# A two-tile decoder step after an expert layer: more of tile 0's second feed-forward under tile 1's expert rows, its down products one at a time in tile 1's gaps

## The chip, the cores and the metric

The kernel runs on one core of a Trainium2 chip, as one program. The metric is the device time of one execution in microseconds; of several executions the median is taken. PE is TensorE, DVE VectorE, ACT ScalarE, POOL GpSimd and SP SyncE. All numbers are 32-bit floats.

## The reference, cut to what matters

There are 256 tokens of width 1024, in two tiles of 128 (tile 0, tile 1). The first block mixes them (retention and attention) and then applies product-key experts: each token picks 16 of 16384 experts in each of 8 heads, and each pick reads a row of `peer_u` and a row of `peer_v`:

```python
u = expert_u[experts]
vsel = expert_v[experts]
act = jax.nn.gelu(jnp.einsum('thkd,td->thk', u, hb), approximate=False)
return jnp.einsum('thk,thkd->td', gate * act, vsel)
```

The second block has two layers. Layer 0 is a short convolution, cross attention to a memory, and a SwiGLU feed-forward (width 2816); layer 1 is block attention, memory attention and a feed-forward again; a norm ends it:

```python
for l in range(DEPTH_2):
    h = rms_norm_2(x, norm_mix[l])
    if l < N_A:
        x = x + short_conv_mixer(h, conv_w_in[l], conv_w[l], conv_w_out[l])
    else:
        x = x + moba_attention(h, ...)
    x = x + mem_cross_attention(...)
    x = x + swiglu(rms_norm_2(x, norm_ffn[l]), ffn_w_gu[l], ffn_w_down[l])
...
return rms_norm_2(x, norm_final)
```

Apart from the block attention of tile 1, which reads keys and values of tile 0, and the convolution's two last columns of tile 0, the tiles don't need each other.

## The kernel before

**The picks.** A pick fetches one row of u and v for each of 128 tokens, 1 MB, with an indirect DMA on POOL's queue (L1602) into one of eight row slots. 16 picks form a group g; picks 0 to 127 are tile 0's, 128 to 255 tile 1's. DVE takes the dot of u with the token (L2064), ACT makes gelu, weight and a small diagonal from it (L1546, L1552, L1559), PE adds diagonal times v into two banks of its own (L1140), and the row slot is free for pick n + 8.

**The layer work.** The second block is cut into steps: `turn`, the norm's transpose of x; `cin`, `q0`, `gu0`, `bk` and so on, products of a tile with one weight block of 2 MB (`layer_unit`, L974: eight matmuls 128x512, each two instructions in the trace); `zturn`, `qturn`, `pturn`, `fturn`, transposes (`layer_turns`, L981); `scores`, `values`, `probs`, `taps`, `rope`, `final`. `gu1 0` to `gu1 10` are the gate and up products of layer 1, eleven blocks; six `fturn1` transposes of their result follow between them; `dn1 0` to `dn1 5` are the down products (L1053), three blocks for each half of x's 1024 columns, the last of each half 1.5 MB. The digit behind a step's name is its layer, the argument its block; a 0 or 1 before it its tile.

**The order.** `STEPS` lists all steps with a cost in us and a lag. The planner (`LAYER_FIRST`, `LAYER_LAST`, `PICK_US`) spreads tile 0's steps over the pick pairs of tile 1, from pair 136 on, at 3.7 us of listed cost for one pick: `PICK_WORK[n]` is what stands before pick pair n on PE, and behind the diagonals of that pair on ACT. DVE does the dots of four picks and then the layer work of both their pairs. Steps planned past pair 252 are `LATE`. That is all of tile 0 from turn ffn1 on. After the rows come tile 1's steps, in order (`AFTER_ROWS`); ahead of each with a lag stands the next late step of tile 0, and the down products of one half go together.

**The weights.** SP loads the blocks in the order in which PE takes them (`SEQUENCE`, L596), into three slots of 2 MB; a slot is free again at the semaphore of the unit that read it last.

**The banks.** Every result of a step is a unit; units take four banks in turn, and PE opens a unit when the one four before it has been read by its engine, DVE or ACT (`UNITS`, `open_unit`). The three down products of one half add up in one bank, and DVE adds it to x once (L2171).

**Names the steps below use.** `add_experts` (L2074) adds the expert sum to x; `tile_x_wait` makes a turn wait for the last addition to x; `f_tok` are the two halves of gated product that `fturn` transposes to `fT`; `oT` holds the attention result for `mo`, `probs` the softmax.

Of the kernel before, what the change touches and what calls it, by code (L numbers as in the profile page):

```python
# [19 lines left out]
D = 1024  # L20
KC = D // P
# [7 lines left out]
MH, BH = 4, 8  # L29
DFF = 2816  # L30
FC = DFF // P
# [171 lines left out]
def feed_steps(l):  # L203

    steps = [(f"turn ffn{l}", 2, 2), (f"root ffn{l}", 0, 0)]
    for j in range(11):
        steps.append((f"gu{l} {j}", 7, 0 if j else 2))
        if j >= 2 and j % 2 == 0:
# [6 lines left out]
         + [("turn blk", 2, 2), ("root blk", 0, 0), ("bk 0", 7, 2), ("bk 1", 7, 0), ("bq 0", 7, 0), ("bq 1", 7, 0), ("bv 0", 7, 0), ("rope 0", 0, 0),  # L215
            ("bv 1", 7, 0), ("kturn 0", 2, 2), ("bqturn 0", 2, 0), ("bscores 0", 2, 2), ("bprobs 0", 0, 2), ("bpturn 0", 2, 2), ("bvalues 0", 3, 2),
            ("bo 0", 7, 2), ("bo 1", 7, 0)] + memory_steps(1) + feed_steps(1) + [("final 0", 0, 2)])
LAYER_FIRST, LAYER_LAST, PICK_US = 136, 252, 3.7
UNDER_ROWS, LATE = [], []
_at, _load = LAYER_FIRST, float(LAYER_FIRST)  # L220
for _w, _us, _lag in STEPS:
    _at = max(_at + _lag, 2 * int(_load // 2))
    _load = max(_load, _at) + _us / PICK_US
    if _at <= LAYER_LAST and not LATE:
        UNDER_ROWS.append(_w)
        PICK_WORK.setdefault(_at, []).append("layer 0 " + _w)
    else:
        LATE.append((_w, _us))
AFTER_ROWS = []
for _w, _us, _lag in STEPS:  # L230
    while _lag and LATE:
        _late, _late_us = LATE.pop(0)
        AFTER_ROWS.append((0, _late))
        if _late_us > 2 and not (_late[:2] == "dn" and _late[-1] not in "25"):
            break
    AFTER_ROWS.append((1, _w))
AFTER_ROWS += [(0, _w) for _w, _ in LATE]
SEQUENCE = [(0, _w) for _w in UNDER_ROWS] + AFTER_ROWS


def units_of(work):

    kind, what = work.split()[:2]
    if kind == "query":
        return [(what, "A")]
    if kind == "keys":
        return [("k" + what, "D")]
    if kind == "regroup":
        return [("g" + what, "D")]
    if kind in ("row", "mean"):  # L250
        return [(what, "D")]
    if kind == "out" and what == "1":
        return [("o1a", "D"), ("o1b", "D")]
    if kind == "repeat":
        return [(f"e{what}a", "A"), (f"e{what}b", "D")]
    if kind == "mkey":
        return [("mk" + what, "A")]
    if kind == "mvalue":
        return [("mv" + what, "A")]
    if kind == "layer":  # L260
        t, step, arg = work.split()[1:]
        late = t == "1"
        return [(n.format(t=t, a=arg, s=step, l=step[-1]), e) for n, e in
                {"turn": [("t{a}{t}0", "D"), ("t{a}{t}1", "A")], "cin": [("ci{t}{a}", "D" if arg in "45" else "A")], "zturn": [("z{t}0", "D"), ("z{t}1", "A")],
# [4 lines left out]
                 "dn": [("dn{l}{t}" + str(int(arg) // 3), "D")] if arg in "25" else [],  # L269
                 "bk": [("bk{t}{a}", "A")], "bq": [("bq{t}{a}", "A")], "bv": [("bv{t}{a}", "A")],  # L270
                 "kturn": [("bkt{t}0", "D"), ("bkt{t}1", "A")], "bqturn": [("bqt{t}0", "D"), ("bqt{t}1", "A")],
                 "bscores": [("bs{t}%d" % i, "D") for i in range(4 if late else 2)],
                 "bpturn": [("bp{t}%d" % i, "DA"[i % 2]) for i in range(4 if late else 2)],
                 "bvalues": [("bw{t}0", "D"), ("bw{t}1", "A")], "bo": [("bo{t}{a}", "D")]}.get(step.rstrip("01"), [])]
    return []
# [21 lines left out]
def units_freed(name, who):  # L297

    return sum(w == who for _, w in UNITS[:unit(name) + 1])
# [22 lines left out]
def build_program(nc, a, out):  # L322
# [5 lines left out]
    with ExitStack() as ctx:  # L328
# [5 lines left out]
        def sem(name):  # L334
            if name not in sems:
                sems[name] = ctx.enter_context(nc.semaphore(name))
            return sems[name]
# [85 lines left out]
        def blocks(v):  # L423
            return v.rearrange("p (k n) -> p k n", n=P)

        def tile_buffers(t):

            def at(t0, t1, n=1024):
                where, c = (t0, t1)[t]
                return where[:, c:c + n]  # L430
# [8 lines left out]
            if t:  # L439
# [2 lines left out]
            heads = 8 * (t + 1)  # L442
            return TileBuffers(
                squares=work, hT=blocks(at((hT_all, 1024), (arena, 3072))), kvT=blocks(first), b_tok=low, z_tok=high, q_tok=low,
                zT=at((h2_all, 0), (arena, 6144), 1040).rearrange("p (k n) -> p k n", k=KC), cvT=blocks(high), qT=blocks(high), oT=blocks(low),
                probs=[v.rearrange("p (h n) -> p h n", h=MH) for v in (first, later)], probs_low=work,
                pT=work.rearrange("p (h k n) -> p h k n", h=MH, k=2),
                sg=[v[:, 0:512].rearrange("p (b n) -> p b n", b=2) for v in (first, later)], f_tok=[v[:, 512:1024] for v in (first, later)], fT=fT, fT4=fT4,
                k_tok=low, bq_tok=high, kq=both.rearrange("p (g n) -> p g n", g=16), rot=work[:, 0:512].rearrange("p (s g n) -> p s g n", s=2, g=16),
# [88 lines left out]
        for name, i, _ in plan:  # L538
            step, t = name[:-1], name[-1]
            if step in ("cin", "cout", "bk", "bq", "bv", "bo"):  # L540
                last_unit[name, i] = {"cin": "ci", "cout": "co"}.get(step, step) + f"{t}{i}"
            elif step[:-1] in ("q", "mo", "gu") and step[-1] in "01":
                last_unit[name, i] = {"q": "lq", "mo": "lo", "gu": "gu"}[step[:-1]] + f"{step[-1]}{t}{i}"
            elif step[:-1] == "dn" and i % 3 == 2:
                last_unit[name, i] = f"{name}{i // 3}"

        def part_read(i):

# [6 lines left out]
        def wait_released(eng, n):  # L555

            name, i, _ = plan[n]
            if name == "mod":
                eng.wait_ge(turn_ready, turn(f"m{i}") + 1)
            elif (name, i) == ("out_again", 1):  # L560
                eng.wait_ge(sem("out_half_used"), 1)
            elif (name, i) in last_unit:
                eng.wait_ge(unit_ready, unit(last_unit[name, i]) + 1)
            elif (name, i) in middle:
                eng.wait_ge(sem("piece_used"), middle.index((name, i)) + 1)
            else:
                assert name[:2] == "dn"
                eng.wait_ge(sem(f"{name}_used"), 2 * (i // 3) + i % 3 + 1)

        def tile_x_wait(eng, t, name, u):  # L570

            if name == "conv":
                eng.wait_ge(experts_added[t], u + 1)
            else:
                eng.wait_ge(unit_free["D"], units_freed({"mem0": "co", "ffn0": "lo0", "blk": "dn0", "mem1": "bo", "ffn1": "lo1", "final": "dn1"}[name] + f"{t}{u}", "D"))

        @block.sync
        def _(sp):
# [26 lines left out]
        def _(pe):  # L605
# [378 lines left out]
            def layer_step(t, step, arg):  # L984
# [49 lines left out]
                                    m = mm(b[:, c - i * 512:c - i * 512 + P], V[:, k, c:c + P], v.pT[:, h, k], start=(k == 0), stop=(k == 1))  # L1034
                        m.then_inc(unit_ready, 1)
                elif kind == "mo":
                    layer_unit(f"lo{l}{t}{arg}", (f"mo{l}{t}", int(arg)), v.oT, f"v{l}{t}0", f"v{l}{t}1")
                elif kind == "gu":
                    layer_unit(f"gu{l}{t}{arg}", (f"gu{l}{t}", int(arg)), v.hT, f"tffn{l}{t}0", f"tffn{l}{t}1")
                elif kind == "fturn":  # L1040
# [2 lines left out]
                    layer_turns(f"ft{l}{t}{m}", [v.f_tok[l][:, c * P:(c + 1) * P] for c in range(4 if m < 5 else 2)])  # L1043
                elif kind == "dn":
                    half, c = divmod(int(arg), 3)
                    if c == 0:
                        open_unit(f"dn{l}{t}{half}", steps_ahead=True)
                    b = bank[unit(f"dn{l}{t}{half}") % 4]
                    w = weights(piece[f"dn{l}{t}", int(arg)])
                    for k in range(8 * c, min(8 * c + 8, FC)):  # L1050
                        if half == 0 and k % 4 == 0:
                            unit_read(f"ft{l}{t}{k // 4}")
                        m = mm(b[:, :], v.fT[k], slot8[w][:, k % 8], start=(k == 0), stop=(k == FC - 1))  # L1053
                    if c == 2:
                        open_unit(f"dn{l}{t}{half}", opened_ahead=True)
                    m.then_inc(unit_ready if c == 2 else sem(f"dn{l}{t}_used"), 1)
                elif kind in ("bk", "bv", "bq"):
                    layer_unit(f"{kind}{t}{arg}", (f"{kind}{t}", int(arg)), v.hT if kind == "bq" else v.kvT, f"tblk{t}0", f"tblk{t}1")
                elif kind == "kturn":
# [105 lines left out]
        def _(act):  # L1165
# [275 lines left out]
            def layer_step(t, step, arg):  # L1441
# [55 lines left out]
                elif kind == "pturn":  # L1497
                    unit_copy(f"pt{l}{t}1", v.probs_low[:, 512:1024])
                elif kind == "values":
                    unit_copy(f"v{l}{t}1", v.oT[:, 4:8])  # L1500
                elif kind == "gu":
                    i, ss, ms, sd, rs = tile_stats(t, f"ffn{l}")
                    j = int(arg)
# [104 lines left out]
        def _(dve):  # L1608
# [504 lines left out]
            def layer_step(t, step, arg):  # L2113
# [48 lines left out]
                elif kind == "bturn":  # L2162
                    for u in range(2):
                        name = f"b{t}{u}"
                        tt(v.cvT[:, 4 * u:4 * u + 4], v.cvT[:, 4 * u:4 * u + 4], unit_in(name)[:, :].rearrange("p (c n) -> p c n", c=4),
                           ALU.mult).then_inc(unit_free["D"], 1)
                elif kind in ("cout", "mo", "bo") or kind == "dn" and arg in "25":
                    half = int(arg) if kind != "dn" else int(arg) // 3
                    name = {"cout": f"co{t}", "mo": f"lo{l}{t}", "bo": f"bo{t}", "dn": f"dn{l}{t}"}[kind] + str(half)
                    c = slice(half * 512, (half + 1) * 512)  # L2170
                    tt(x[:, t, c], x[:, t, c], unit_in(name)[:, :], ALU.add).then_inc(unit_free["D"], 1)  # L2171
                elif kind == "qturn":
                    unit_copy(f"qt{l}{t}0", v.qT[:, 0:4])
# [10 lines left out]
                elif kind == "pturn":  # L2184
                    unit_copy(f"pt{l}{t}0", v.probs_low[:, 0:512])
                elif kind == "values":
                    unit_copy(f"v{l}{t}0", v.oT[:, 0:4])
                elif kind == "gu":
                    i, ss, ms, sd, rs = tile_stats(t, f"ffn{l}")
                    j = int(arg)  # L2190
# [113 lines left out]
```

## Time and profile before

| | us |
|---|---|
| median of 3 runs | 1830.45 |
| lowest, highest | 1827.85, 1831.81 |
| the profiled execution | 1836.24 |
| its span in the trace | 1834.4 |
| mean granted clock of PE | 0.946 |
| PE busy in it | 1623.2 (88%) |
| DVE busy | 738.1 (40%) |
| ACT busy | 484.9 (26%) |
| moved by DMA | 595.21 MB |

The profiled execution stands 5.8 us above the median of the others. Times in rows are microseconds from the start of its span. A row of the timeline is a run of like instructions: start, length, engine and line, what it writes and reads, how many; in brackets, the idle time of the engine just before it and what ended it. A matmul overlaps the next, so the time of a step is read from its start to the start of the one behind it.

### The profile page before, as it was taken

The numbers are of one execution on the slowest core, as the hardware profiler recorded it, in microseconds if no ns is written. First come the engines' busy times: TensorE is split into PE (matmuls) and PEld (weight loads), VectorE is DVE, ScalarE is ACT, GpSimd is POOL, SyncE is SP. The second block draws the span as 40 slices with busy tenths as digits, with TensorE's granted clock in tenths as the row PEclk, the third lists the DMA queues.
The fourth block names the chain that finished last, engine by engine and source line by source line (L and its number), as shares of the span: only waits on it lengthen the run. The fifth ranks groups of instructions, "written<-read, shape, count | busy, mean of one in ns | idle before, by whom it ended". The sixth has DMA issues, their size and how long they took to land.

```text
span 1834.4 us, 15459 instructions
## 1 busy us (share of the span) xinstructions
PE 1623.2 (88%) x5460; PEld 755.6 (41%) x5460; DVE 738.1 (40%) x1784; ACT 484.9 (26%) x1267; POOL 277.5 (15%) x268
## 2 busy tenths in 40 slices
PE   6998998498569998898799999789999999989998
PEld 3444464174134442233333333244445444455443
DVE  3653146866584555746635445451101010031000
ACT  3311223323222323323443323332112011122110
POOL 1000002333243323322312222320000000000000
PEclk8998999799889998899899999899999999999999
DMA  9545337999999999999999999996776677764674
GB/s 354 193 156 183 121 143 312 412 377 417 421 388 371 399 421 417 413 421 421 417 375 420 422 420 422 420 387 227 288 281 257 263 304 280 301 237 183 255 295 183
DMA packets 94956, 595.21 MB, mean 324 GB/s; under 512 B 7024, under 2 KB 7024, under 8 KB 28192
## 3 DMA queue, kind: packets, MB, share of 16 engines
q1 hardware_dynamic: 56576, 319.28, 44.9%
q0 software_dynamic: 37584, 270.75, 36.1%
q10 hardware_dynamic: 720, 4.19, 0.6%
q8 instruction: 44, 0.72, 0.2%
q14 instruction: 32, 0.26, 0.0%
HBM read 593.15 MB, written 1.05 MB: 324 GB/s over the span
## 4 chain that ended last, share of the span: by engine, by line
PE 76%; DMA 9%; DVE 8%; ACT 4%; issue 2%; POOL 1%; DVEq 0%; SPq 0%; ACTq 0%; POOLq 0%
PE bank L974 35%; PE bank L1140 9%; PE bank L1053 8%; PE bank L684 6%; DMA arena<-in_peer_rows,pidx 6%; PE bank L946 3%; DVE arena L2064 3%; DMA ring<-in_w_mod 2%; PE bank L937 2%; PE bank L761 2%; PE bank L981 2%; PE bank L738 1%; PE bank L781 1%; PE bank L1034 1%; PE bank L656 1%
## 5 line engine op out<-in xcount | busy, mean ns | idle before, releaser
L1602 POOL DMA_INDIRECT arena<-in_peer_rows,pidx x256 | 272.6, 1065 | 921.2 <-PE bank L1140 603.3
L1140 PE MATMUL bank<-arena,keep 128*32 128x512 f32 x1024 | 277.6, 691 | 128.5 <-ACT keep L1559 128.4
L2064 DVE SCALAR_TENSOR_TENSOR arena<-arena,ring 128x1024 f32<-128x1024 f32 x256 | 304.8, 1221 | 165.1 <-DMA arena<-in_peer_rows,pidx 163.8
L974 PE MATMUL bank<-ring,arena 128*128 128x512 f32 x736 | 319.3, 592 | 1.1 <-issue 1.1
L974 PE MATMUL bank<-ring,hT_all 128*128 128x512 f32 x544 | 242.4, 601 | 4.9 <-issue 2.6
L974 PEld LDWEIGHTS bank<-ring,arena 128*128 128x128 f32 x736 | 138.7, 190 | 170.8 <-issue 170.8
L1140 PEld LDWEIGHTS bank<-arena,keep 128*32 128x32 f32 x1024 | 52.3, 119 | 300.2 <-ACT keep L1559 168.6
L974 PEld LDWEIGHTS bank<-ring,hT_all 128*128 128x128 f32 x544 | 102.4, 192 | 137.3 <-issue 137.2
L2171 DVE TENSOR_TENSOR x_all<-x_all,bank 128x512 f32<-128x512 f32 x24 | 16.5, 687 | 224.2 <-PE bank L1053 125.7
L1546 ACT ACTIVATE pf<-pf 128x2 f32<-128x2 f32 x128 | 25.8, 201 | 302.9 <-DVE arena L2064 302.7
L684 PE MATMUL bank<-ring,hT_all 128*128 128x512 f32 x192 | 89.0, 621 | 3.0 <-DVE hT_all L1679 3.0
L1053 PE MATMUL bank<-ring,arena 128*128 128x512 f32 x176 | 75.9, 592 | 0.0
L1559 ACT ACTIVATE keep<-keep,pf 128x32 f32<-128x32 f32 x256 | 68.2, 313 | 4.2
L2194 DVE SCALAR_TENSOR_TENSOR arena<-bank,stat,arena 128x256 f32<-128x256 f32 x22 | 10.6, 484 | 137.9 <-ACT arena L1508 137.9
L1552 ACT ACTIVATE pf<-pf,grouped 128x1 f32<-128x1 f32 x256 | 61.4, 287 | 4.2
L761 PE MATMUL bank<-hT_all,ring 128*128 128x128 f32 (+1 forms) x384 | 60.6, 317 | 0.3 <-ACT hT_all L1175 0.3
L684 PEld LDWEIGHTS bank<-ring,hT_all 128*128 128x128 f32 x192 | 38.0, 201 | 51.3 <-issue 51.3
L974 PE MATMUL bank<-ring,s_all 128*128 128x512 f32 x128 | 55.9, 595 | 3.4 <-issue 3.4
L761 PEld LDWEIGHTS bank<-hT_all,ring 128*128 128x128 f32 x384 | 55.0, 197 | 8.9 <-issue 5.6
L937 PE MATMUL bank<-mem_all,ring 128*128 128x256 f32 x256 | 58.3, 386 | 0.0
L946 PE MATMUL bank<-ring,mem_all 128*128 128x512 f32 x128 | 57.0, 598 | 0.0
L1053 PE MATMUL bank<-ring,s_all 128*128 128x512 f32 x128 | 56.2, 595 | 0.1
(365 smaller groups left out, 1551.3 us busy)
## 6 DMA issues: line engine op xcount, KB each, us to landing
ring<-in_weights SPq DMA_DIRECT2D x126, 2048.0 KB
ring<-in_w_mod SPq DMA_DIRECT2D x12, 2048.0 KB
ring<-in_w_in SPq DMA_DIRECT2D x6, 2048.0 KB
ring<-in_weights SPq DMA_DIRECT2D x8, 1024.0 KB
arena<-in_peer_rows,pidx POOLq DMA_INDIRECT x256
ring<-in_weights SPq DMA_DIRECT2D x8, 512.0 KB
mem_all<-in_b_mod POOLq DMA_DIRECT2D x3, 512.0 KB, 9.7
hT_all<-in_xT ACTq DMA_DIRECT2D x1, 1024.0 KB, 7.6
```

What stands on the lines that cost most here:

```text
L684: m = mm(b[:, :], src[:, k, t * P:(t + 1) * P], slot8[w][:, k], start=(k == 0), stop=(k == KC - 1))
L761: m = mm(b[:, s * n:(s + 1) * n], slot8[w][:, k, c:c + P], hT[:, k, cols_of], start=(k == 0), stop=(k == KC - 1))
L937: m = mm(bk[:, b * TOK:(b + 1) * TOK], slot8[w][:, k, (2 * half + b) * P:(2 * half + b + 1) * P], memT[l][:, k], start=(k == 0), stop=(k = ...
L946: m = mm(b[:, :], memT[l][:, k, t * P:(t + 1) * P], slot4[w][:, k % 4, half * 512:(half + 1) * 512], start=(k == 0), stop=(k == KC - 1))
L974: m = mm(b[:, :], src[:, k], slot8[w][:, k], start=(k == 0), stop=(k == KC - 1))
L981: i = tr(b[:, c * P:(c + 1) * P], src, ident)
L1053: m = mm(b[:, :], v.fT[k], slot8[w][:, k % 8], start=(k == 0), stop=(k == FC - 1))
L1140: m = mm(acc[b][r:r + 32, :], diag[n % 8], vslot[n % SLOTS][:, b * 512:(b + 1) * 512], start=(n % 128 < 4), stop=(n % 128 >= 124))
L1552: m = f(pw2[:, c + k:c + k + 1], pgel2[:, c + k:c + k + 1], ACT.Copy, scale=grouped[:, g % 4, i % 4, 1, i // 4:i // 4 + 1])
L1559: f(diag[n % 8], eq32, ACT.Copy, scale=pw2[:, c + k:c + k + 1]).then_inc(sem("diag_ready"), 1)
L1602: nc.gpsimd.indirect_dma_start(out=row_in[n % SLOTS], out_offset=None, in_=a["peer_rows"], in_offset=bass.IndirectOffsetOnAxis(ap=pidx[:, ...
L2064: stt(uslot[n % SLOTS], uslot[n % SLOTS], 1.0, h2g[n % 4], ALU.mult, ALU.mult, accum_out=pact2[:, 16 * (g % 2) + k:16 * (g % 2) + k + 1]). ...
```

## The change

`LAYER_LAST` goes, `PICK_US` is 5.2, and the planner places every step of tile 0 under the rows but the six `dn1` and `final`. All steps from pair 144 on stand closer: turn mem0 before pair 152 instead of 156, turn blk before 196 instead of 212, and turn ffn1, all of gu1 and fturn1 before pairs 234 to 252. After the rows the seven steps left stand where `FILLS` says: one down product each ahead of tile 1's turn conv, cin 2, turn mem0, probs0, turn ffn0 and turn blk, and the norm ahead of tile 1's gu1 3. Each down product, of both tiles and layers, is now a unit with a bank and an addition to x of its own. `oT` and `probs` of layer 1 take other parts of the buffers.

```diff
-LAYER_FIRST, LAYER_LAST, PICK_US = 136, 252, 3.7
-UNDER_ROWS, LATE = [], []
+LAYER_FIRST, PICK_US = 136, 5.2
+UNDER_ROWS, DOWN = [], [f"dn1 {c}" for c in range(6)]
 _at, _load = LAYER_FIRST, float(LAYER_FIRST)
 for _w, _us, _lag in STEPS:
     _at = max(_at + _lag, 2 * int(_load // 2))
     _load = max(_load, _at) + _us / PICK_US
-    if _at <= LAYER_LAST and not LATE:
+    if _w not in DOWN + ["final 0"]:
+        assert _at < 256
         UNDER_ROWS.append(_w)
         PICK_WORK.setdefault(_at, []).append("layer 0 " + _w)
-    else:
-        LATE.append((_w, _us))
+FILLS = {"turn conv": ["dn1 0"], "cin 2": ["dn1 1"], "turn mem0": ["dn1 2"], "probs0 0": ["dn1 3"], "turn ffn0": ["dn1 4"], "turn blk": ["dn1 5"],
+         "gu1 3": ["final 0"]}
 AFTER_ROWS = []
 for _w, _us, _lag in STEPS:
-    while _lag and LATE:
-        _late, _late_us = LATE.pop(0)
-        AFTER_ROWS.append((0, _late))
-        if _late_us > 2 and not (_late[:2] == "dn" and _late[-1] not in "25"):
-            break
-    AFTER_ROWS.append((1, _w))
-AFTER_ROWS += [(0, _w) for _w, _ in LATE]
+    AFTER_ROWS += [(0, _fill) for _fill in FILLS.get(_w, ())] + [(1, _w)]
...
-                 "dn": [("dn{l}{t}" + str(int(arg) // 3), "D")] if arg in "25" else [],
+                 "dn": [("dn{l}{t}{a}", "D")],
...
                 elif kind == "dn":
                     half, c = divmod(int(arg), 3)
-                    if c == 0:
-                        open_unit(f"dn{l}{t}{half}", steps_ahead=True)
-                    b = bank[unit(f"dn{l}{t}{half}") % 4]
                     w = weights(piece[f"dn{l}{t}", int(arg)])
-                    for k in range(8 * c, min(8 * c + 8, FC)):
+                    ks = range(8 * c, min(8 * c + 8, FC))
+                    b = open_unit(f"dn{l}{t}{arg}")
+                    for k in ks:
                         if half == 0 and k % 4 == 0:
                             unit_read(f"ft{l}{t}{k // 4}")
-                        m = mm(b[:, :], v.fT[k], slot8[w][:, k % 8], start=(k == 0), stop=(k == FC - 1))
-                    if c == 2:
-                        open_unit(f"dn{l}{t}{half}", opened_ahead=True)
-                    m.then_inc(unit_ready if c == 2 else sem(f"dn{l}{t}_used"), 1)
+                        m = mm(b[:, :], v.fT[k], slot8[w][:, k % 8], start=(k == ks[0]), stop=(k == ks[-1]))
+                    m.then_inc(unit_ready, 1)
...
-                elif kind in ("cout", "mo", "bo") or kind == "dn" and arg in "25":
-                    half = int(arg) if kind != "dn" else int(arg) // 3
+                elif kind in ("cout", "mo", "bo", "dn"):
+                    half = int(arg) // (3 if kind == "dn" else 1)
...
+                    if kind == "dn" and arg not in "03":
+                        copied(f"dn{l}{t}{int(arg) - 1}")
                     tt(x[:, t, c], x[:, t, c], unit_in(name)[:, :], ALU.add).then_inc(unit_free["D"], 1)
```

## Rows read from the trace of the kernel before

**Rows 1.** The page: busy time, and DMA in forty slices of the span
```profile
PE 1623.2 (88%) x5460; PEld 755.6 (41%) x5460; DVE 738.1 (40%) x1784; ACT 484.9 (26%) x1267; POOL 277.5 (15%) x268
...
DMA  9545337999999999999999999996776677764674
GB/s 354 193 156 183 121 143 312 412 377 417 421 388 371 399 421 417 413 421 421 417 375 420 422 420 422 420 387 227 288 281 257 263 304 280 301 237 183 255 295 183
```

**Rows 2.** Windows: under tile 1's rows, after them, and a part of the first
```profile
core 0: us, PE busy (x) PEld busy (x) DVE busy (x) ACT busy (x) POOL busy (x), PEclk, DMA share, GB/s
...
750.70:1251.70 501.00, 449.55 (x1401) 180.78 (x1397) 243.22 (x580) 173.61 (x470) 120.31 (x112) 0.95 0.98 406
1251.70:1834.40 582.70, 557.90 (x1540) 268.17 (x1538) 71.16 (x164) 94.65 (x193) 0.00 (x0) 0.99 0.69 260
...
1075.20:1184.00 108.80, 93.79 (x293) 37.37 (x291) 51.94 (x115) 35.24 (x105) 26.91 (x24) 0.91 1.01 421
```

**Rows 3.** Windows: the last 22 us of the stretch under the rows
```profile
1230.00:1240.00 10.00, 10.00 (x47) 6.26 (x46) 5.36 (x9) 3.03 (x11) 0.00 (x0) 0.91 0.46 190
1240.00:1252.00 12.00, 12.00 (x42) 4.81 (x42) 1.49 (x3) 0.00 (x0) 0.00 (x0) 1.00 0.54 189
```

**Rows 4.** DMA issues by line, with their size
```profile
ring<-in_weights SPq DMA_DIRECT2D x126, 2048.0 KB
```

**Rows 5.** Waits from 750 to 1252 us: total, times, longest
```profile
PE bank L1140 <- ACT keep L1559: 44.0, 16, 6.7
```

**Rows 6.** Timeline of PE under the rows: cout, two pick pairs, bpturn
```profile
817.09 13.97 PE L974 MATMUL bank<-ring,s_all 128*128 128x512 f32 x32 [2.92 <-issue]
...
911.99 3.63 PE L1140 MATMUL bank<-arena,keep 128*32 128x512 f32 x8 [6.67 <-ACT keep L1559]
...
1158.43 1.97 PE L981 MATMUL bank<-keep,s_all 128*128 128x128 f32 x8 [2.71 <-DVE s_all L2232]
...
1234.01 1.91 PE L1140 MATMUL bank<-arena,keep 128*32 128x512 f32 x8
```

**Rows 7.** Timeline of PE after the rows, where tile 0's late steps stand
```profile
1251.65 1.09 PE L981 MATMUL bank<-keep,x_all 128*128 128x128 f32 x8
1255.33 8.80 PE L974 MATMUL bank<-ring,hT_all 128*128 128x512 f32 x16 [2.59 <-issue]
1263.97 1.04 PE L981 MATMUL bank<-keep,x_all 128*128 128x128 f32 x8
...
1306.92 7.03 PE L974 MATMUL bank<-ring,arena 128*128 128x512 f32 x16
1313.79 7.03 PE L974 MATMUL bank<-ring,hT_all 128*128 128x512 f32 x16
...
1321.53 0.60 PE L981 MATMUL bank<-keep,s_all 128*128 128x128 f32 x4
1322.97 7.10 PE L974 MATMUL bank<-ring,hT_all 128*128 128x512 f32 x16 [0.84 <-DVE s_all L2194]
...
1414.75 3.73 PE L1034 MATMUL bank<-arena,mem_all 128*128 128x128 f32 x32
```

**Rows 8.** Timeline of PE in tile 1's layer 1, with nothing of tile 0
```profile
1665.52 0.60 PE L981 MATMUL bank<-keep,x_all 128*128 128x128 f32 x4
...
1667.11 13.97 PE L974 MATMUL bank<-ring,arena 128*128 128x512 f32 x32
1680.92 0.60 PE L981 MATMUL bank<-keep,arena 128*128 128x128 f32 x4
...
1682.35 3.69 PE L1018 MATMUL bank<-mem_all,arena 128*128 128x256 f32 x16
...
1689.58 5.29 PE L1034 MATMUL bank<-arena,mem_all 128*128 128x128 f32 x32
1694.70 13.90 PE L974 MATMUL bank<-ring,arena 128*128 128x512 f32 x32
```

**Rows 9.** The page: DVE's additions of a product to x
```profile
L2171 DVE TENSOR_TENSOR x_all<-x_all,bank 128x512 f32<-128x512 f32 x24 | 16.5, 687 | 224.2 <-PE bank L1053 125.7
```

More of the change, by code:

```diff
@@ L444, in tile_buffers @@
                 squares=work, hT=blocks(at((hT_all, 1024), (arena, 3072))), kvT=blocks(first), b_tok=low, z_tok=high, q_tok=low,
-                zT=at((h2_all, 0), (arena, 6144), 1040).rearrange("p (k n) -> p k n", k=KC), cvT=blocks(high), qT=blocks(high), oT=blocks(low),
-                probs=[v.rearrange("p (h n) -> p h n", h=MH) for v in (first, later)], probs_low=work,
+                zT=at((h2_all, 0), (arena, 6144), 1040).rearrange("p (k n) -> p k n", k=KC), cvT=blocks(high), qT=blocks(high), oT=[blocks(low), blocks(high)],
+                probs=[v.rearrange("p (h n) -> p h n", h=MH) for v in (first, low)], probs_low=work,
                 pT=work.rearrange("p (h k n) -> p h k n", h=MH, k=2),
@@ L541, in build_program @@
                 last_unit[name, i] = {"cin": "ci", "cout": "co"}.get(step, step) + f"{t}{i}"
[L542 to L545, printed above, removed]
+            elif step[:-1] in ("q", "mo", "gu", "dn") and step[-1] in "01":
+                last_unit[name, i] = {"q": "lq", "mo": "lo"}.get(step[:-1], step[:-1]) + f"{step[-1]}{t}{i}"
         def part_read(i):
@@ L563, in wait_released @@
                 eng.wait_ge(unit_ready, unit(last_unit[name, i]) + 1)
-            elif (name, i) in middle:
+            else:
                 eng.wait_ge(sem("piece_used"), middle.index((name, i)) + 1)
-            else:
-                assert name[:2] == "dn"
-                eng.wait_ge(sem(f"{name}_used"), 2 * (i // 3) + i % 3 + 1)
         def tile_x_wait(eng, t, name, u):
@@ L574, in tile_x_wait @@
             else:
-                eng.wait_ge(unit_free["D"], units_freed({"mem0": "co", "ffn0": "lo0", "blk": "dn0", "mem1": "bo", "ffn1": "lo1", "final": "dn1"}[name] + f"{t}{u}", "D"))
+                eng.wait_ge(unit_free["D"], units_freed({"mem0": "co{t}{u}", "ffn0": "lo0{t}{u}", "blk": "dn0{t}{d}", "mem1": "bo{t}{u}", "ffn1": "lo1{t}{u}",
+                                                              "final": "dn1{t}{d}"}[name].format(t=t, u=u, d=3 * u + 2), "D"))
         @block.sync
@@ L1036, in layer_step @@
                 elif kind == "mo":
-                    layer_unit(f"lo{l}{t}{arg}", (f"mo{l}{t}", int(arg)), v.oT, f"v{l}{t}0", f"v{l}{t}1")
+                    layer_unit(f"lo{l}{t}{arg}", (f"mo{l}{t}", int(arg)), v.oT[l], f"v{l}{t}0", f"v{l}{t}1")
                 elif kind == "gu":
@@ L1499, in layer_step @@
                 elif kind == "values":
-                    unit_copy(f"v{l}{t}1", v.oT[:, 4:8])
+                    unit_copy(f"v{l}{t}1", v.oT[l][:, 4:8])
                 elif kind == "gu":
@@ L2166, in layer_step @@
                            ALU.mult).then_inc(unit_free["D"], 1)
-                elif kind in ("cout", "mo", "bo") or kind == "dn" and arg in "25":
-                    half = int(arg) if kind != "dn" else int(arg) // 3
-                    name = {"cout": f"co{t}", "mo": f"lo{l}{t}", "bo": f"bo{t}", "dn": f"dn{l}{t}"}[kind] + str(half)
+                elif kind in ("cout", "mo", "bo", "dn"):
+                    half = int(arg) // (3 if kind == "dn" else 1)
+                    name = {"cout": f"co{t}", "mo": f"lo{l}{t}", "bo": f"bo{t}", "dn": f"dn{l}{t}"}[kind] + arg
                     c = slice(half * 512, (half + 1) * 512)
+                    if kind == "dn" and arg not in "03":
+                        copied(f"dn{l}{t}{int(arg) - 1}")
                     tt(x[:, t, c], x[:, t, c], unit_in(name)[:, :], ALU.add).then_inc(unit_free["D"], 1)
@@ L2186, in layer_step @@
                 elif kind == "values":
-                    unit_copy(f"v{l}{t}0", v.oT[:, 0:4])
+                    unit_copy(f"v{l}{t}0", v.oT[l][:, 0:4])
                 elif kind == "gu":
```

## The prediction

> **What bounds the kernel now.** I read the page first, then split the span where the structure of the kernel does. The page says that PE is busy for 1623.2 us, 88% of the span, so the idle 12%, some 210 us, is all that can be won by moving work; and that from the fifteenth to the twenty-sixth of forty slices the transfers run at one flat rate, 413 to 422 GB/s but for one slice at 375 [rows 1]. So there are two regimes. The windows give them apart. From 750.7 us (pick pair 138, where tile 0's layer work starts) to 1251.7 us (the last pick) PE is busy 449.55 of 501.0 us and the DMA engines 0.98 of the time: this stretch is bound by transfers. From there to the end PE is busy 557.90 of 582.7 us and DMA only 0.69, at 260 GB/s: this one is bound by PE [rows 2]. The reader should see that PE has about 51 us free in the first, and DMA about a third of its time free in the second. The change moves eleven 2 MB blocks, with their products, out of the stretch that has DMA to spare into the one that has none. Whether it pays is a comparison of two prices for the same work, its bytes and its PE time.
>
> The chain of waits agrees: in the first stretch PE waits 44.0 us for the diagonals of ACT, which wait for DVE's dots, which wait for rows [rows 5]. In the second, units follow each other at 6.87 us, the distance between the start of one and the start of the next [rows 7].
>
> **The second stretch, what leaves.** Turn ffn1 and gu1 0 take from 1251.65 to 1263.97, 12.3 us, with 2.59 of idle among them [rows 7]. Ten further gu1 units are 10 x 6.87 = 68.7 us. The six transposes of tile 0's f_tok cost, from the start of each to the start of the work behind it, 1.44 us (1321.53 to 1322.97 [rows 7]) where DVE is awaited; four more places of this kind give 1.32, 1.32, 0.44 and 1.83 us, 6.35 us together. Sum 87.4 us. The six products of dn1 stay in this stretch and keep their time.
>
> **The second stretch, what comes back.** The moved work had filled tile 1's waits. The same steps of tile 1's other layer have no filler and price them [rows 8]. Turn mem runs 1.59 us from its start to that of q (1665.52 to 1667.11) against the 0.87 us of eight transposes without a wait, so +0.72; bturn is built alike, +0.72. Qturn takes 1.43 us (1680.92 to 1682.35), +0.56, and pturn, with dn1 3 now ahead of it, +0.56 likewise. Values take 5.12 us (1689.58 to 1694.70) where they took some 3.6 us filled (the 3.73 us row of [rows 7]), +1.55. Together 4.1 us. Turn blk gains a filler, -0.6. I take +3.5; its bounds are 0 (the new fillers cover all) and about 7 (bturn as dear as cout's 2.92 us wait [rows 6], values with another 1 us). That tile 1's first turn waits for the experts' sum costs nothing: dn1 0, one unit of 6.87 us, covers it, and it is the 2.59 us that gu1 0 paid before. The stretch shrinks by 87.4 - 3.5 = **84 us**.
>
> **The first stretch, what is added.** Eleven blocks of 2.097 MB [rows 4] are 23.1 MB. At 421 GB/s, the rate that holds there [rows 1], they cost **54.8 us**. In PE time the same work is 11 x 6.87 + 6.35 = 81.9 us with its turns, more than the 51 us of idle, so PE alone asks for at least 31 us more; the bytes ask for more and decide. That needs both to fit: 449.6 + 82 = 532 us of PE work in a stretch of about 556 us is 96%, which is tight, but the 532 holds picks at the lower clock (3.63 us for a pair after 6.67 us of idle, against 1.91 us [rows 6]), which shrink as the waits for rows do.
>
> Two corrections. First the tail: behind the last row's landing DMA does 190 GB/s for 22 us [rows 3], 12 us of lost transfer. In the new order PE has two units, three short turns and four pick pairs, 13.7 + 1.5 + 7.6 = 23 us, behind the last row's issue, where it had 26; I take -3 us. Second the order: DVE reads units only after the dots of a group of four rows, so a step whose input DVE made in the same group waits for two rows more. Reading the planned places, 11 such steps stood under the rows before, and 17 do now, since steps now fall one pair apart (zturn, cout, q, scores, pturn, mo, gu0 0, two of fturn0, bk, kturn, bvalues, turn mem1, values1, turn ffn1, two of fturn1). PE's two longest waits at the old ones are 2.92 us at cout and 2.71 us at bpturn [rows 6], and the fturns in such places carry no idle in PE's timeline; at a little under 1 us each for six more, +5 us. The bounds of the whole term: below, every idle moment of DMA used up, (203.4 + 23.1) MB / 421 = 538 us, +37; above, PE's 51 us of idle all kept and its 82 us added, +82. I take 54.8 - 3 + 5 = **+57**, nearer to the lower end because transfers ran at 0.98 in this stretch already.
>
> Here a rule of the Trainium skill speaks against the change. The page's slices show 421 GB/s for hundreds of microseconds on end [rows 1]. DMA: Bandwidth & Descriptors, Where 436 GB/s comes from, says that for transfers from HBM the limit is the HBM side, about 358 GB/s for a core; by it the 23.1 MB would be an estimated 64 us and not 55, and the gain 9 us smaller. The trace disagrees with it as a ceiling, and the measured rate is used.
>
> **Edits at nothing.** Sixteen more additions of a down piece to x, eight of them under the rows, are 16 x 0.687 = 11 us of DVE [rows 9], which is idle half of the first stretch and seven eighths of the second; the very last addition is the same as before. Uncovered, the eight under the rows would cost 5.5 us. Weight slots of dn come free at the same matmul as before. Each piece now takes a bank of its own, and a bank is asked for again four units later, some 27 us. Final 0 puts about 3 us of ACT and 2.5 us of DVE under one gu1 unit of tile 1 that lasts 6.87 us; its stores stay at the end of SP's queue. POOL issues the same 256 rows. The moved blocks pass nothing on SP's queue but each other, and share the engines with the rows, which is the 54.8 us.
>
> **Sum.** -84 + 57 = -27 us. The profiled execution took 1836.2 us (span 1834.4), so a profiled run of the new kernel should be near 1809; it stands 5.8 us above the median of the three runs, 1830.45, and against that the forecast is **1803 us**. A measurement of this kernel can tell about 0.2% (3.7 us) from no change.
>
> **The rivals.**
> *Idle transfers are used up (0.12).* Denser PE work frees slots evenly and DMA never stops but for a short tail: about +42 instead of +57, so 1788. For it: PE's clock rises when waits vanish. Against: what idle there was came when PE was the slower one, which will be more common.
> *PE's idle stays (0.10).* The waits under the rows are of order and not of bytes, and the 82 us simply add: -84 + 82 = -2, so 1828; a little of it used gives 1825. For it: 96% use of two engines with eight row slots and three weight slots between them. Against: DMA at 1.01 for stretches of 109 us on end [rows 2].
> *The groups of four bind; slower (0.08).* PE stands at the 17 steps listed, units behind it cannot run, weight slots stay full and DMA stops too. It decides from a total of 43 us, 2.5 us a step (27 + 5 + some 11 paid now). With 4.4 us each, between the 2.9 of the longest such wait and the 6.67 us of the longest wait for a diagonal [rows 6], it is 17 x 4.4 - 11 = 64 us in place of 5: 1862. Against it: the fturns in such places show no wait now.
> *The rate falls with more weights in the mix (0.05).* Two slices, the twelfth and thirteenth, gave 388 and 371 GB/s with DMA at nine tenths or more [rows 1]; at 371 the bytes cost 62 us: 1810. The skill's 358 points this way.
> *The change does less than it says (0.03).* Tile 1's bare waits cost four times my 3.5 us, since fillers stand in the wrong places: 1814.
> The forecast itself has 0.62, with its own range 1791 to 1816.
>
> **Numbers.** The range 1787 to 1822 takes in the forecast, the first rival, the last two and part of the second; what is left out is most of the second and the slower one, under 2 in 10. Faster by over 0.2% (below 1826.8): 0.62 + 0.12 + 0.05 + 0.03 and 0.04 of the second, 0.86. Same: the rest of it, 0.06. Slower: 0.08.
>
> **What the new profile would show.** The last pick moves from 1251 to about 1308 us; the stretch before it holds 226 MB at over 400 GB/s with PE idle down from 51 to some 30 us; the rest lasts about 499 us with PE at 96% or more and DMA lower than before; picks of 3.6 us become rarer. Wrong it would be if that stretch grows past 575 us with DMA below 0.93 (order, not bytes), or if the rest is over 510 us (bare waits).

## The result, and the profile after

The kernel after takes 1821.8 us in the median against 1832.2 for the kernel before: ratio 0.994, interval 0.9928 to 0.9952, some 11 us faster. The forecast was 27 us. One of its 18 executions took 5606.5 us and is left out of the ratio. The profiled execution took 1821.5 us, where the one of before stands 4 us above its median. The page of the kernel after, the parts that answer to [rows 1]:

```profile
span 1819.7 us, 15512 instructions
...
PE 1620.8 (89%) x5460; PEld 754.2 (41%) x5460; DVE 748.3 (41%) x1800; ACT 502.0 (28%) x1279; POOL 288.1 (16%) x268
...
DMA  9545237999999999999899999999977577754774
GB/s 355 200 154 185 115 152 307 406 383 417 421 395 372 402 420 416 421 421 391 344 386 401 421 421 386 421 405 421 369 268 281 211 293 271 301 228 185 264 291 183
```

PE's work is the same, its idle time fell by 12 us. The flat rate of DMA now has a hole at the nineteenth to twenty-second slice (391, 344, 386, 401), where the kernel before had one slice at 375. I cut the span at the same steps as before: turn conv of tile 0 at 748.6 us (752.5 before), the last pick at 1317.4 (1251.7). The windows, with the columns of [rows 2], are the whole stretch under the rows, the rest of the span, and then the stretch by tile 0's parts. Each part is named after the turn it begins with: conv, mem0, ffn0, blk, mem1, ffn1.

```profile
748.60:1317.40 568.80, 527.67 (x1602) 216.83 (x1600) 250.26 (x598) 204.11 (x506) 123.32 (x112) 0.96 0.98 401
1317.40:1819.70 502.30, 479.67 (x1334) 233.31 (x1332) 73.71 (x162) 79.48 (x165) 0.00 (x0) 0.98 0.67 252
748.60:823.00 74.40, 72.55 (x213) 29.88 (x211) 34.45 (x93) 18.97 (x55) 14.78 (x14) 0.99 1.01 421
823.00:893.40 70.40, 57.49 (x204) 25.59 (x202) 36.48 (x93) 25.00 (x68) 18.76 (x16) 0.93 0.92 363
893.40:1047.90 154.50, 148.20 (x413) 58.57 (x411) 62.82 (x154) 55.15 (x119) 30.67 (x28) 0.98 0.98 400
1047.90:1150.50 102.60, 90.56 (x285) 36.91 (x283) 53.85 (x129) 36.25 (x106) 26.43 (x22) 0.92 0.99 405
1150.50:1213.40 62.90, 56.92 (x204) 25.58 (x202) 33.55 (x77) 23.82 (x68) 15.70 (x16) 0.92 1.01 412
1213.40:1317.40 104.00, 101.96 (x296) 40.29 (x294) 29.12 (x54) 44.92 (x92) 17.00 (x16) 0.98 0.97 402
```

Counted from turn conv in both, the stretch grew from 499.2 to 568.8 us, +70 where +57 was forecast, and the rest fell from 582.7 to 502.3, -80 where -84 was forecast: -11 in all, which is what the medians say. Inside the stretch PE's busy time rose by 80 us (447.75 in the same cut of before) and its idle time fell only from 51 to 41 us. The part mem0 stands out: PE is idle for 13 of 70 us and DMA runs at 363 GB/s. Both wait there, so a third must be late.

It is DVE. Waits in the stretch of the kernel after, and below them the one of before that compares with the second row (total, times, longest):

```profile
PE bank L1128 <- ACT keep L1547: 41.1, 14, 7.0
DVE arena L2052 <- DMA arena<-in_peer_rows,pidx: 19.2, 8, 7.8
```
```profile
DVE arena L2064 <- DMA arena<-in_peer_rows,pidx: 61.0, 32, 4.0
```

PE waits for the picks' diagonals nearly as long as before (41.1 against 44.0 us [rows 5]), but DVE waits for rows only a third as long (19.2 against 61.0). So most rows have landed, and their dots are late. The longest of PE's waits, at pick pair 160, in the timeline of the kernel after (start, length, engine, line; in brackets idle time and what ended it):

```profile
847.38 0.69 DVE L1629 COPY s_all<-bank 128x512 f32<-128x512 f32 x1 [8.42 <-PE bank L972]
...
853.88 0.69 DVE L2166 TENSOR_REDUCE small<-bank 128x2 f32<-128x512 f32 x1 [5.80 <-PE bank L1009]
...
856.41 0.17 DVE L1969 TENSOR_SCALAR ptop<-ptop 128x16 uint32<-128x16 uint32 x1
...
860.45 0.29 DVE L1986 TENSOR_TENSOR s_all<-comb,keep 128x128 f32<-128x128 f32 x1
860.66 1.22 DVE L2052 SCALAR_TENSOR_TENSOR arena<-arena,ring 128x1024 f32<-128x1024 f32 x1
...
863.82 0.53 ACT L1547 ACTIVATE keep<-keep,pf 128x32 f32<-128x32 f32 x2
...
864.40 3.63 PE L1128 MATMUL bank<-arena,keep 128*32 128x512 f32 x8 [7.00 <-ACT keep L1547]
868.80 0.94 POOL L1590 DMA_INDIRECT arena<-in_peer_rows,pidx  x1 [8.45 <-PE bank L1128]
```

DVE waits 8.4 us for PE in qturn and 5.8 us in scores, the layer work of the two pairs of one group; then it does 4.2 us of picking for a later group (L1969 to L1986); then the dots of rows 160 to 163, without a wait for them. PE has nothing left from 857.4 to 864.4, and the pick behind it runs at 3.63 us instead of 1.91. POOL, which gets its slots from that pick, issues no row for 8.45 us. The DMA rate falls with it:

```profile
860.00:870.00 10.00, 5.59 (x20) 2.38 (x22) 7.66 (x21) 2.52 (x11) 1.30 (x2) 0.66 0.69 283
```

That is one place of the hole; the rest of it, up to 1000 us, is not traced to single waits here.

### The profile page after: what moved, and what is told of

It is laid out like the page before. It is cut to its first block, busy times and chain, and to the rows that moved or that the text cites. A ratio compares the mean times of both kernels' runs of the same rounds, so it can differ in the third digit from the quotient of the medians.

```text
span 1819.7 us, 15512 instructions
## 1 busy us (share of the span) xinstructions
PE 1620.8 (89%) x5460; PEld 754.2 (41%) x5460; DVE 748.3 (41%) x1800; ACT 502.0 (28%) x1279; POOL 288.1 (16%) x268
## 4 chain that ended last, share of the span: by engine, by line
PE 76%; DVE 9%; DMA 8%; ACT 4%; issue 2%; POOL 1%; DVEq 0%; SPq 0%; ACTq 0%; POOLq 0%
PE bank L965 34%; PE bank L1128 10%; PE bank L1043 8%; PE bank L675 6%; DMA arena<-in_peer_rows,pidx 6%; PE bank L937 3%; DVE arena L2052 3%; PE bank L928 2%; PE bank L752 2%; DMA ring<-in_w_mod 2%; PE bank L972 2%; PE bank L729 1%; PE bank L647 1%; PE bank L1025 1%; POOL arena L1590 1%
## 5 line engine op out<-in xcount | busy, mean ns | idle before, releaser
L1590 POOL DMA_INDIRECT arena<-in_peer_rows,pidx x256 | 283.2, 1106 | 979.2 <-PE bank L1128 662.7
L2161 DVE TENSOR_TENSOR x_all<-x_all,bank 128x512 f32<-128x512 f32 x40 | 27.5, 688 | 225.9 <-PE bank L1043 124.2
```

The costliest lines, as they stand in the source:

```text
L1590: nc.gpsimd.indirect_dma_start(out=row_in[n % SLOTS], out_offset=None, in_=a["peer_rows"], in_offset=bass.IndirectOffsetOnAxis(ap=pidx[:, ...
```

## The experiments

All are timed against the kernel before on the same chip, in five rounds. A ratio is to that kernel, and a difference in us between two runs is worked out from their ratios. First the two parts of the change that can stand alone, and the bytes.

**singles** and **dense_only**. Both have the products and buffers of the kernel after and the interleaving of the one before. singles keeps its planner; dense_only plans densely and stops at mo1 1, so that the last eleven pick pairs stand alone.

```diff
 # dense_only, against singles
-LAYER_FIRST, LAYER_LAST, PICK_US = 136, 252, 3.7
+LAYER_FIRST, LAYER_LAST, PICK_US = 136, 232, 5.2
```

> The kernel before with two parts of the change alone: each down product a unit of its own with its own addition to x, and the new places of oT and probs. The planner is that of before. Forecast's theory (edits at nothing): 1832 us, ratio to before 1.000 within 0.002. Rival (sixteen more additions and banks hold PE or DVE up, 0.7 us each where bare): up to 11 us more, 1843, ratio 1.006.

> Density alone: tile 0's steps stand as close under the rows as after the change (the same pairs up to mo1 1 before pair 232), but turn ffn1, gu1 and fturn1 stay behind the rows, interleaved as before, so that the last eleven pick pairs have no layer work. Bytes theory (the stretch under the rows costs its bytes at 421 GB/s): no more bytes, so 1832, ratio 1.000. Order theory (DVE stands in layer work while landed rows wait for their dots, and DMA stops): some 9 us of DMA idle more in the pairs up to 232, 1841, ratio 1.005.

Measured: singles 1832.8 us, ratio 0.9995 (0.9981 to 1.001): sixteen additions and the banks cost nothing, as forecast. dense_only 1849.1 us, ratio 1.0094 (1.0072 to 1.0116): 17 us slower with no more bytes under the rows. The windows show the stretch and the part of it up to 1200 us; below them are PE's waits for the diagonals up to there:

```profile
746.80:1262.40 515.60, 452.96 (x1397) 181.03 (x1395) 245.51 (x584) 170.59 (x464) 126.70 (x112) 0.93 0.97 397
746.80:1200.00 453.20, 415.13 (x1281) 172.52 (x1280) 219.83 (x542) 158.43 (x414) 107.63 (x96) 0.95 0.98 401
```
```profile
PE bank L1133 <- ACT keep L1552: 38.1, 12, 7.0
```

The stretch is 16.4 us longer than in the kernel before, with the same bytes within 1% (397 x 515.6 against 406 x 499.2). Its first 453 us look like those of the kernel after, the longest wait of 7.0 us included. Density has a price of its own, almost twice what I had expected of it here, and more than three times the 5 us of the forecast.

**half_gu1**. Of each gu1 block of tile 0 only half is loaded; the second half of these products uses old weights. PE does the same work.

```diff
+        if name == "gu10":
+            plan.append((name, i, [(a["weights"][n, 0], 0, RUN)]))
+            return
```

> The kernel after, but of each of the eleven gu1 blocks of tile 0 only the first half (1 MB) is loaded, so the second half of the product uses old weights: 11.5 MB less are moved under the rows, PE's work is the same. Bytes theory: 11.5 MB / 421 GB/s = 27 us less, 1794, ratio to before 0.979. PE-bound or order theory (PE is busy 102 of 104 us in the part that holds gu1): 0 to 6 us less, 1816 to 1821, ratio 0.991 to 0.994.

Measured: 1822.6 us, ratio 0.9936 (0.9912 to 0.9959), the same as the kernel after within the interval. The stretch, and the part with gu1:

```profile
751.30:1320.20 568.90, 526.70 (x1602) 217.33 (x1600) 249.91 (x598) 203.81 (x506) 122.48 (x112) 0.96 0.95 380
1216.00:1320.20 104.20, 102.17 (x296) 40.41 (x294) 29.11 (x54) 45.01 (x92) 16.95 (x16) 0.98 0.83 311
```

568.9 us in place of 568.8, 104.2 in place of 104.0, with DMA at 311 instead of 402 GB/s. So the bytes did not bind this part. PE did: it was busy for 102 of the 104 us.

**lead**. The kernel after with DVE's dots always one pick pair ahead of its layer work.

```diff
+            dotted = [0]
+
-            def dots(g, q):
-                for k in range(4 * q, 4 * q + 4):
-                    n = 16 * g + k
+            def dots(g, q, ahead=0):
+                for n in range(dotted[0], min(16 * g + 4 * q + 4 + ahead, 16 * PK)):
+                    dotted[0] = n + 1
+                    g, k = divmod(n, 16)
...
                     for n in (16 * g + 4 * q, 16 * g + 4 * q + 2):
+                        if g >= 8 and n % 4 == 2:
+                            dots(g, q, 2)
```

> The kernel after, with DVE's dots always one pick pair ahead of its layer work (from pick 128 on the two dots of the next pair come before the layer work of the second pair of each group of four rows), nothing else moved. Order theory: the picks' waits on ACT (41 us in 14 waits after the change, of which only 19 us of DVE's waits are for rows) shrink, the stretch of 569 us loses 8 to 12 us, 1811, ratio to before 0.989. Bytes theory: its bytes are the same, 1821, ratio 0.994.

Measured: 1798.9 us, ratio 0.9814 (0.9791 to 0.9838), the fastest kernel here that leaves nothing out, 34 us ahead of the one before and 23 of the one after; twice what I had expected. The stretch, and its parts ffn0, blk and ffn1, in lead; then its waits:

```profile
744.50:1296.60 552.10, 516.47 (x1603) 214.59 (x1601) 252.25 (x600) 205.80 (x511) 122.72 (x112) 0.98 1.01 415
...
886.40:1033.80 147.40, 145.47 (x413) 58.03 (x411) 62.72 (x154) 55.28 (x120) 30.10 (x28) 1.00 1.01 418
1033.80:1134.20 100.40, 87.11 (x285) 35.98 (x283) 52.60 (x126) 34.34 (x101) 23.70 (x22) 0.95 1.01 420
...
1195.00:1296.60 101.60, 100.52 (x297) 40.09 (x295) 27.96 (x54) 44.77 (x92) 17.86 (x16) 1.00 1.00 413
```
```profile
PE bank L1128 <- ACT keep L1547: 22.0, 7, 8.2
DVE arena L2055 <- DMA arena<-in_peer_rows,pidx: 50.7, 28, 4.0
```

PE's wait for diagonals is halved, and DVE waits for rows again: 31.4 of the 50.7 us stand in part blk, where DMA ran at 420 GB/s. Of the 17 us that the stretch lost, 11 are PE's busy time (527.7 to 516.5) and 6 its idle time. I had counted only the second kind. Most of the 11 is in the picks, as the windows of their line alone show, in the kernel after and in lead (PE and PEld only):

```profile
748.60:1317.40 568.80, 124.56 (x474) 23.48 (x472) 0.96 0.98 401
744.50:1296.60 552.10, 115.72 (x474) 22.61 (x472) 0.98 1.01 415
```

The remaining 6 of the 23 us lie outside the stretch: it starts 4.1 us earlier, and what follows it is 1.9 us shorter. That start scatters between 741 and 753 us over these kernels, so whether the 4.1 us are the early dots' is open.

**lead_before** and **lead_dense**: the same edit on the kernel before and on dense_only.

> The kernel before, with the dots one pick pair ahead as in lead. Order theory: in the kernel before the rows were the bottleneck (DVE waited 61 us for them), DMA idle was only 18 us of the stretch, so at most half of it comes back, 1824 to 1832, ratio 0.995 to 1.000; then the change on top of the early dots is worth 26 to 33 us, what its bytes and PE times had promised. Rival (the early dots are a gain of their own, whatever the placing): 22 us here too, 1811, ratio 0.988.

> Density alone (dense_only, 1.0094 of before), with the dots one pick pair ahead. Order theory: what density cost was DVE's place for the dots, and it goes: ratio to before 0.997 to 1.001, 1827 to 1834. Rival (steps one pair apart starve each other whatever DVE does): 1.005 or more stays, 1841.

Measured: lead_before 1829.9 us, 0.9979 (0.9965 to 0.9993); lead_dense 1831.1 us, 0.9988 (0.9972 to 1.0003). The early dots are worth 4 us without the change and 23 with it. With early dots in both, density costs one or two us instead of 17 (0.9988 against 0.9979). And the change is then worth 0.9814 / 0.9979 = 0.983, 30 us, the size that the forecast had given it.

**lead_half_gu1** and **lead_half_gu0**: is it the bytes that bind now? Lead, with half of each gu1 block of tile 0, or of each gu0 block, left out as in half_gu1.

> Lead, with only half of each gu1 block of tile 0 loaded (the second half of the product uses old weights). In lead the stretch moves 229 MB in 552 us, 544 us of it at 421 GB/s, and PE is busy 95.5 of the last 96.6 us. If bytes bind the whole stretch now: 11.5 MB / 421 GB/s = 27 us less, 1772, ratio to before 0.966. If the part with gu1 is bound by PE, whatever the bytes: 0 to 5 us less, 1794 to 1799, ratio 0.979 to 0.982.

> Lead, with only half of each of the eleven gu0 blocks of tile 0 loaded (the second half of those products uses old weights): 11.5 MB less in the part from tile 0's turn conv to its turn ffn1, which in lead took 450.5 us at 416 GB/s with PE busy 93% of it. If bytes bind this part in lead: 11.5 MB / 421 GB/s = 27 us at most, and as PE's own waits then come first, 10 to 25 us less than lead, 1774 to 1789, ratio to before 0.968 to 0.976. If order or PE binds it still, as in the part with gu1, where halving did nothing: 0 to 3 us, 1796 to 1801, ratio 0.980 to 0.983.

Measured: 1801.6 us, 0.9829 (0.9802 to 0.9855), and 1798.9 us, 0.98 (0.9779 to 0.9822): lead's time in both. For gu0 the expectation was 10 to 25 us if bytes bind and 0 to 3 if not, and DMA had run at 1.01 in its part; it is the second. The window of lead_half_gu0 about that part:

```profile
890.00:1045.00 155.00, 151.56 (x436) 60.51 (x433) 68.91 (x170) 61.80 (x136) 35.30 (x32) 1.00 0.92 358
```

DMA falls to 358 GB/s and the part keeps its length, 147.4 us from turn ffn0 to turn blk in both kernels. DMA at full rate was no bottleneck there; it was only never out of work. Nor did the saving reach the next, light part: from turn blk to turn mem1 lead takes 100.4 us and lead_half_gu0 100.7. My reading is that eight row slots and three weight slots can't hold it; no run changes the slots. So in the two product-heavy parts tested half of a block's bytes are free, and the block's price is PE's 6.87 us. No run takes bytes from a light part, and in lead's blk, with DMA at 420 GB/s and DVE waiting for rows, they may well bind.

**chosen_first**, **first138**: two other ways to change what stands ahead of the dots, on the kernel after. In chosen_first DVE's picking stands ahead of the group's layer work, not behind it. In first138 the planner starts one pair later, so every step of tile 0 stands one pick pair later on all engines.

```diff
 # chosen_first: these two blocks of DVE's loop change places
-                    for n in (16 * g + 4 * q, 16 * g + 4 * q + 2):
...
                     if 0 < g < 14:
                         if q < 2:
                             half_top(g + 2, q)
...
+                    for n in (16 * g + 4 * q, 16 * g + 4 * q + 2):
...
 # first138
-LAYER_FIRST, PICK_US = 136, 5.2
+LAYER_FIRST, PICK_US = 138, 5.2
```

> The kernel after, with DVE's picking of later experts (half_top, best_pairs, pair_rows, spread, 1.8 to 4.3 us for each group of four rows) moved ahead of the layer work of the group, where DVE waits for PE, instead of between it and the next dots. Order theory: the dots after six or seven of the groups come 2 to 4 us sooner, PE's wait of 7.0 us at pair 160 among them, 10 to 15 us in all, 1809, ratio 0.987. If only the position of the dots against the layer work counts, and not what stands between: 0 to 3 us, 1820, ratio 0.993.

> The kernel after, with every step of tile 0 one pick pair later (the planner starts at 138 instead of 136), so that each stands in the other half of its group of four rows. The forecast's rule counted steps whose input DVE makes in the same group: 17 before the shift, 16 after it; by it the time stays, 1821, ratio 0.993 to 0.995. If what counts is which light steps (turns, scores, probs) stand second in a group, ahead of the next dots, the waits move: the 7.0 us at pair 160 goes and others come, a difference of 4 us or more either way, with no bytes changed.

Measured: chosen_first 1814.0 us, 0.9889 (0.9868 to 0.991); first138 1812.9 us, 0.9887 (0.9866 to 0.9908). Each is 9 to 10 us faster than the kernel after, with the same bytes and the same products. PE's order is the same in chosen_first; in first138 the layer steps keep their order but stand between other picks. chosen_first lies between its two expectations, 10 to 15 us and 0 to 3. Their waits for diagonals, chosen_first and first138:

```profile
PE bank L1128 <- ACT keep L1547: 22.9, 9, 8.4
```
```profile
PE bank L1128 <- ACT keep L1547: 34.9, 12, 5.9
```

A shift by one pair is worth as much as most of the change. My count of steps that stand with their input in one group of four (17, and 16 after the shift) said that it was worth nothing. Which of the moved steps bring the 10 us is open.

**lead_fill3** and **both_fill3**. One place in the rest of the program: dn1 3 was meant to cover the softmax of tile 1's mem0. lead_fill3 is lead with dn1 3 behind DVE's scaling of the probabilities; both_fill3 is that with chosen_first's order as well. The timeline of PE there, in the kernel after:

```profile
1415.11 7.03 PE L1043 MATMUL bank<-ring,s_all 128*128 128x512 f32 x16
1423.65 1.38 PE L972 MATMUL bank<-keep,arena 128*128 128x128 f32 x8 [1.51 <-DVE arena L2173]
1425.13 5.44 PE L1025 MATMUL bank<-arena,mem_all 128*128 128x128 f32 x32
```

```diff
-         "probs0 0": ["dn1 3"]
+         "pturn0 0": ["dn1 3"]
```

> Lead, with tile 0's dn1 3 ahead of tile 1's pturn0 instead of ahead of probs0: PE's order stays the same, but DVE scales the probabilities during the product and adds it to x behind, where in the change it adds first and PE waits 1.5 us for the probabilities. Theory of the queue on DVE: 1.5 us less, 1797.5 against lead's 1799, near the limit of the measurement; in the trace the wait of 1.5 us between dn1 3 and pturn is gone. Rival (the product covers it anyway and the 1.5 us are of another wait): the same wait stays.

> All that helped: lead, chosen_first and dn1 3 behind DVE's scaling of the probabilities. In lead the stretch under the rows ran 544 of its 552 us at the full rate of DMA, so if the two cures are one, 1795 to 1799, ratio 0.980 to 0.982. If chosen_first's 9 us are of another kind and add up: 1789, ratio 0.976.

Measured: lead_fill3 1800.3 us, 0.9817 (0.9794 to 0.984), no difference in time that can be told from lead; both_fill3 1802.6 us, 0.983 (0.9805 to 0.9855), so what chosen_first brings does not add to lead. But the wait for DVE is gone in the timeline of lead_fill3:

```profile
1390.52 7.03 PE L1043 MATMUL bank<-ring,s_all 128*128 128x512 f32 x16
1397.39 1.04 PE L972 MATMUL bank<-keep,arena 128*128 128x128 f32 x8
1398.98 3.81 PE L1025 MATMUL bank<-arena,mem_all 128*128 128x128 f32 x32 [0.55 <-issue]
```

From the end of the product to values it is now 1.6 us, where lead and the kernel after have 3.15. PE's order is the same in both; DVE had the product's addition to x ahead of the probabilities in its queue, and waited for the product before it scaled them.

## Why the prediction was right or wrong

**The step that failed** is the first stretch's term, +57 = 54.8 - 3 + 5. It measured +70.

The term that was mis-sized is the +5 us for order. dense_only, which has the density and not the moved blocks, lengthened the stretch by 16.4 us (499.2 to 515.6). The kernel after stands another 53.2 us above it (568.8), where 54.8 - 3 = 52 was forecast for the moved blocks. So 11 of the missing 13 us are order's, as far as the two can be added.

The 54.8 us for the bytes came near in size by luck, for they were the price of something that did not bind. Half of the moved bytes taken away changed neither the part (104.2 against 104.0 us) nor the time. I had read the bound from a mean: DMA at 0.98 over 501 us. By parts it is another matter. Under the dense plan PE is busy for 72.6 of 74.4, 148 of 154.5 and 102 of 104 us of the product-heavy parts, and half of gu0's bytes are as free in lead as half of gu1's. The two prices nearly tie in the part with gu1: it moved 402 GB/s x 104.0 us = 41.8 MB, which at 421 GB/s is an estimated 99 us against PE's 102. What fits the runs is PE's account: 80 us more of busy time, as the prediction had it (82), less the idle time that the work took up, which was 10 us and not the 25 that +57 implies. Nor did the picks shrink, as the prediction thought: PE's time for them in the stretch was 123.9 us before and 124.6 after.

On order the prediction saw one half of the mechanism (DVE reads a unit only after the dots of its group) and looked for its price at the steps that wait for DVE. Most of it is paid at the picks: DVE waits for PE inside the layer work, and the dots of rows that have landed queue behind it. It costs 17 us in dense_only, nearly all of which the early dots give back, and lead is 23 us faster than the kernel after, against 4 us for the same edit on the kernel before. Nor did the count of places say anything, as the shift by a pair shows. The -3 us for the tail I could not check by itself.

**The rivals.** The one that PE's idle stays (1828, chance 0.10) was nearest in kind: 41 of 51 us stayed. The result, 11 us, lies between it and the forecast. In the rival of the groups of four the mechanism was partly right: in part mem0 DMA fell to 363 GB/s while PE and DVE waited for each other. But at 17 us it makes a smaller gain and not a slower kernel. Idle transfers weren't used up: 401 GB/s against 406. The rate did not fall by the mix of queues: slices at 420 and 421 GB/s still stand in the stretch, and part conv runs at 421. By that the Trainium skill's figure of some 358 GB/s (DMA: Bandwidth & Descriptors, Where 436 GB/s comes from) is again not the ceiling of this core; where 358 does appear, in lead_half_gu0, half of the block bytes had been left out of a part that ran at 418 with them.

**The second stretch** came near, -80 for -84. The filler of turn blk brought nothing (2.26 us from turn to bk, 2.19 before), and pturn cost 3.15 us from the end of dn1 3, 1.5 of it for DVE's queue; the prediction had priced both by PE's order alone. The other bare waits were as priced (turn mem0 1.66 us, qturn 1.44).

**Edits at nothing** cost nothing (singles, 0.9995). The prediction put eight of the sixteen added additions under the rows; the trace has four there (10 before, 14 after, line L2161), which changes nothing in the sum. **What would prove it wrong** was set at a stretch past 575 us with DMA below 0.93; at 569 us and 0.98 for the whole, neither showed, though the miss was one of order: a mean over the stretch hid the 70 us in which DMA ran at 0.92.

That the forecast's 27 us and the 30 us of lead against lead_before agree is no proof of its working: in lead too, half of the blocks' bytes in the product-heavy parts could go without a change in time.

## What to carry to other kernels

Ask of a full DMA queue whether anything waits for it: halve the bytes and look. Work that serves two streams in order on one engine (here dots for the picks, copies for the layers) should do the feeding stream's part first, one step ahead, before it enters steps that wait for the bound engine. Here a plan that packs the steps more closely made that order cost more. And a filler on PE covers a wait only if the engine that PE waits for does not have to handle the filler's result first.

## What the runs showed of the hardware that was not expected

A pair of picks takes 1.91 us or up to 3.63 us by what stood before it. That was half of what the early dots brought back in the stretch: the picks' time fell by 8.8 of its 16.7 us, at a granted clock of 0.98 instead of 0.96. The clock row shows this only as a mean. The rule that PE falls to its lower clock in waits for transfers and pays at the next matmuls (the Trainium skill, TensorE: Matmul & The Clock Gate, HAM oscillation) agrees with the 3.63 us behind 7.00 us of idle, though the wait here was for a diagonal, and with 1.91 us where picks follow other work.
